# Earlier modulations, and side work begun by a credit of VectorE time, in a two-block transformer kernel

## The reference

```
mod = silu(c) @ w_ada + b_ada                    # 2048 x 12288: sh1, sc1, gt1, sh2, sc2, gt2
h = rmsnorm(x) * (1 + sc1) + sh1
qa, ka, va, qb, kb, vb, q_idx, k_idx, w_idx, ga, gb = split(h @ w_in)
ya = causal attention A (8 heads) @ w_moba_out
yb = attention B (8 heads), keys chosen by an index (top 64 a query) @ w_dsa_out
y = (sigmoid(ga) * ya + sigmoid(gb) * yb) @ w_o
x = x + gt1 * rmsnorm(y);  h = rmsnorm(x) * (1 + sc2) + sh2
x = x + gt2 * rmsnorm(relu(h @ w_ff1)^2 @ w_ff2)
# the second block has two other attentions and a second feed-forward, and no modulation
```

## Time and profile before

| | |
|---|---|
| timed runs | 2645.92, 2650.81, 2651.06 us, median 2650.81 |
| profiled execution | 2645.48 us, span 2643.7 us, mean granted clock 0.99 |
| PE busy | 2572.5 us (97%) |
| DVE busy | 1712.8 us (65%) |
| ACT busy | 1212.1 us (46%) |
| chain that ended last | PE 85%, DVE 10%, ACT 3% |
| HBM read | 563.02 MB, 214 GB/s over the span |

### The profile page before, as it was taken

The page is one execution under the profiler, slowest core; times in us unless marked ns, Lnnn a source line. Parts: engine busy times, 40 slices in busy tenths (PEclk is TensorE's granted clock), DMA queues, the critical chain, the costliest instruction groups (busy, mean ns, idle before and its releaser), DMA issues.

```text
span 2643.7 us, 30528 instructions
## 1 busy us (share of the span) xinstructions
PE 2572.5 (97%) x12368; PEld 2124.6 (80%) x12368; DVE 1712.8 (65%) x2256; ACT 1212.1 (46%) x1766; POOL 5.9 (0%) x15
## 2 busy tenths in 40 slices
PE   6999998999998999999999989999999999999998
PEld 4887786887886888888888878878778888888887
DVE  5897878878885866556556554546655465564555
ACT  3534444534346434434444455445554344443443
POOL 0000000000000000000000000000000000000000
PEclk8999999999999999999999999999999999999999
DMA  8994345788885775555555535534445555555553
GB/s 332 381 348 167 128 150 213 268 339 325 337 328 191 265 292 207 193 189 188 195 188 180 210 131 188 193 129 144 175 151 197 180 188 197 185 191 194 187 193 143
DMA packets 80443, 567.10 MB, mean 215 GB/s; under 512 B 8976, under 2 KB 9104, under 8 KB 15664
## 3 DMA queue, kind: packets, MB, share of 16 engines
q1 hardware_dynamic: 79200, 558.09, 57.8%
q0 software_dynamic: 1104, 7.07, 0.7%
HBM read 563.02 MB, written 2.10 MB: 214 GB/s over the span
## 4 chain that ended last, share of the span: by engine, by line
PE 85%; DVE 10%; ACT 3%; issue 1%; DMA 1%; DVEq 0%; SPq 0%; ACTq 0%
PE ps L884 19%; PE ps L881 19%; PE ps L882 18%; PE ps L925 15%; PE ps L927 8%; DVE wl L1545 4%; DVE ACC L1566 2%; DMA raw<-stream_in 1%; ACT wh L1192 1%; PE ps L941 1%; PE ps L1134 1%; DVE TMP L1671 1%; ACT M L1323 1%; DVE M L1675 1%; PE ps L1110 1%
## 5 line engine op out<-in xcount | busy, mean ns | idle before, releaser
L1545 DVE TENSOR_TENSOR wl<-raw,wh 128x1024 fp32r<-128x1024 f32 x851 | 1003.6, 1220 | 573.3 <-ACT wh L1192 572.8
L1192 ACT ACTIVATE wh<-raw 128x1024 fp32r<-128x1024 f32 x851 | 852.5, 1049 | 726.7 <-PE ps L884 555.1
L925 PE MATMUL ps<-HT,wh 128*128 128x512 f32 x1792 | 634.3, 399 | 0.0
L881 PE MATMUL ps<-wh,U 128*128 128x512 f32 x1376 | 538.1, 391 | 0.0
L884 PE MATMUL ps<-wl,U 128*128 128x512 f32 x1376 | 536.3, 390 | 1.4 <-DVE wl L1545 1.4
L882 PE MATMUL ps<-wh,U 128*128 128x512 f32 x1376 | 535.5, 389 | 0.0
L927 PE MATMUL ps<-HT,wl 128*128 128x256 f32 x1792 | 503.4, 281 | 0.5 <-DVE wl L1545 0.5
L881 PE MATMUL ps<-wh,HT 128*128 128x512 f32 x1120 | 451.0, 403 | 18.7 <-ACT wh L1192 10.2
L884 PE MATMUL ps<-wl,HT 128*128 128x512 f32 x1120 | 445.9, 398 | 12.3 <-DVE wl L1545 12.0
L882 PE MATMUL ps<-wh,HT 128*128 128x512 f32 x1120 | 441.9, 395 | 0.0
L925 PEld LDWEIGHTS ps<-HT,wh 128*128 128x128 f32 x1792 | 336.6, 188 | 83.0 <-DVE M L1912 0.2
(11 more groups left out here) (234 smaller groups left out, 1315.3 us busy)
## 6 DMA issues: line engine op xcount, KB each, us to landing
raw<-stream_in SPq DMA_DIRECT2D x497, 1024.0 KB, 4.8
raw<-stream_in SPq DMA_DIRECT2D x16, 896.0 KB, 7.3
raw<-stream_in SPq DMA_DIRECT2D x17, 640.0 KB, 6.6
raw<-stream_in SPq DMA_DIRECT2D x13, 512.0 KB, 4.7
M<-rows_in POOLq DMA_DIRECT2D x6, 1024.0 KB, 5.9
X<-x_in SPq DMA_DIRECT2D x2, 1024.0 KB, 7.1
y_out<-X SPq DMA_DIRECT2D x4, 512.0 KB, 2.6
CT<-consts_in POOLq DMA_DIRECT2D x1, 376.0 KB, 6.8
```

The lines of the kernel that those rows point to most:

```text
L881: e.matmul(o, ah, H[:, c:c + bw], start=k == k0, stop=False)
L925: e.matmul(o[:, :], H[:, c], a.rearrange("p h n -> p (h n)"), start=k == 0, stop=False)
L1192: e.activation(H, raw[place[n][0]][:, c:c + w], ACT.Copy).then_inc(*hi.tick(p))
L1545: e.tensor_tensor(L, raw[place[n][0]][:, c:c + w], H.bitcast(F32), ALU.subtract).then_inc(*lo.tick(p))
```

## The change

At the start, all four quarters of the second pair's modulation stand ahead of the first chunk's banks on TensorE, and the stream takes the first chunk's load behind two of them; the column sums of that pair come before the last of the four banks. The "a" events take another order of columns and begin in the third phase: eleven there, the other 37 spread over qA to wo0 by a count for each slab. The slabs from qi@2 to wo0 (kiwi apart) write their side steps with `paced()`: a step is written only while a credit is above zero. The credit grows by 1.5 for each piece, shrinks by 2.6 for each modulation load, by a cost for the slab's evacuation and by a cost for each step; at most 4.0 is carried from chunk to chunk. At most two steps are written per chunk. kA's ropes are queued ahead of attention B.

```diff
@@ plan
-    for j in range(2):
-        out += [("p", j, i) for i in range(4)]
-        if j == 0:
-            out.append(chunks.pop(0))
+    out += [("p", 0, i) for i in range(4)] + [("p", 1, 0), ("p", 1, 1), chunks.pop(0), ("p", 1, 2), ("p", 1, 3)]
...
-    mixed(["qi@2", "kiwi", "qB@2", "kB@2", "vB@2", "kA@2", "vA@2"], [], 1)
-    ada = [("a", c, j) for c in (3 * D, 3 * D + 1024, 2 * D, 2 * D + 1024, 4 * D, 4 * D + 1024) for j in range(8)]
-    mixed(["qA", "gb0", "yb0", "gb1", "yb1", "ga0", "ya0", "ga1", "ya1", "wo0", "wo1"], ada, 1, ADA_SKIP, True)
+    chunks = phase(2)
+    chunks.insert(4, ("g", "kiwi", 0))
+    ada = [("a", c, j) for c in (3 * D, 3 * D + 1024, 4 * D, 2 * D, 2 * D + 1024, 4 * D + 1024) for j in range(8)]
+    beside(chunks, ada, (0, 1, 0, 0, 0) + 5 * (1, 1, 0, 0))
+    for name, n in (("qA", 4), ("gb0", 3), ("yb0", 2), ("gb1", 4), ("yb1", 2), ("ga0", 6), ("ya0", 2), ("ga1", 6),
+                    ("ya1", 2), ("wo0", 6), ("wo1", 0)):
+        m = len(slab_chunks(name))
+        beside([("g", name, i) for i in range(m)], ada, [(i + 1) * n // (m - 1) - i * n // (m - 1) if i < m - 1 else 0
+                                                         for i in range(m)])
@@ work_order
+SIDE_COST = {"rope": 2.1, "attention": 0.6, "index": 1.0, "turnx": 0.3, "rot": 1.0, "srow": 2.3}
+EVAC_COST = {"qi": 2.7, "qB": 2.7, "kB": 2.7, "vB": 2.7, "kA": 2.7, "vA": 2.7, "qA": 1.3, "yb": 2.8, "ya": 5.6, "wo": 2.8}
 FIRST_EVAC = {"qA": ("index",), "gb0": ("attention", "B"), "v2": ("attention", "M")}
...
+    def paced():
+
+        while side and side[0][1] == segments(side[0][0]):
+            side.popleft()
+        if side and at["credit"] > 0:
+            at["credit"] -= SIDE_COST.get(side[0][0][0], 0.3)
             steps(1)
...
-            hooks = {(0, nb - 1): lambda: steps(max(1, rate // 2))}
+            hooks = {(0, nb - 1): paced if pace else lambda: steps(max(1, rate // 2))}
...
+            if name.partition("@")[0] in FIRST:
+                for k in pieces[ps[0]]["ks"] + pieces[ps[-1]]["ks"]:
+                    finish("turnx", max(x for x, q in enumerate(X_TILES) if q[0] <= k))
+            for task in NEEDS.get((name, i), ()):
+                finish(*task)
+            if pace:
+                width_us = width / 1024
+                at["credit"] = min(at["credit"], 4.0) + (2.7 - 1.2) * width_us * sum(len(pieces[p]["ks"]) for p in ps)
+                at["credit"] -= 2.6 * (nx - n - many)
+                if i + many == total:
+                    at["credit"] -= EVAC_COST.get(name[:2], 0.0) if name[-2:] != "@0" else 0.0
...
-            if hooks is not tail:
+            if pace:
+                paced()
+            elif hooks is not tail:
                 steps(rate // 2)
...
-    first_mods(0, 0)
-    split(4)
+    first_sums(0, 1, 2, 3)
+    add("rowcopy", 3)
+    colsum(3)
+    first_sums(4)
+    add("xhalves", 0)
+    split(6)
+    first_sums(5, 7, 8)
     for t in range(2):
         for b in range(2):
-            add("bank", "qi@0", parts[4], t, b, True, False)
-    at["done"] = parts[4][-1]
-    first_mods(1, 5)
+            if (t, b) == (1, 1):
+                add("rowcopy", 8)
+                colsum(8)
+            add("bank", "qi@0", parts[6], t, b, True, False)
+    at["done"] = parts[6][-1]
+    add("xhalves", 1)
...
-    run("qi@2")
+    run("qi@2", pace=True)
     later("rope", "qi")
     run("kiwi")
     later("ki")
     later("index")
     for name in FIRST[1:]:
-        run(f"{name}@2", 2)
-    later("rope", "qB")
-    later("rope", "kB")
+        run(f"{name}@2", pace=True)
+    for name in ("qB", "kB", "kA"):
+        later("rope", name)
     later("attention", "B")
-    run("qA", 2)
+    run("qA", pace=True)
     later("rope", "qA")
-    later("rope", "kA")
     later("attention", "A")
     for s in range(2):
-        run(f"gb{s}", 2 - s)
-        run(f"yb{s}")
+        run(f"gb{s}", pace=True)
+        run(f"yb{s}", pace=True)
...
+NEEDS = {("wo0", 4): [("mix", 1)], ("wo0", 7): [("srow", "mix")], ("fd00", 0): [("gm", "f", 0, 0)],
+         ("gd00", 0): [("gm", "g", 0, 0)]}
```

More of the change, by code:

```diff
@@ L27 @@
 RING = 4
-ADA_SKIP = 10
 MAGIC = 12582912.0
@@ L124, in plan @@
     assert not columns
-    mixed(["qi@2", "kiwi", "qB@2", "kB@2", "vB@2", "kA@2", "vA@2"], [], 1)
-    ada = [("a", c, j) for c in (3 * D, 3 * D + 1024, 2 * D, 2 * D + 1024, 4 * D, 4 * D + 1024) for j in range(8)]
-    mixed(["qA", "gb0", "yb0", "gb1", "yb1", "ga0", "ya0", "ga1", "ya1", "wo0", "wo1"], ada, 1, ADA_SKIP, True)
+    chunks = phase(2)
[7 more added lines that the diff above has]
+                                                         for i in range(m)])
+    assert not ada
     mixed([f"f{p}{g}{s}" for g in range(4) for p in "ud" for s in range(2)],
@@ L262, in work_order @@
     side, held, pending, tiles = deque(), deque(), [], deque()
-    at = {"pos": 0, "ring": 0, "done": None}
+    at = {"pos": 0, "ring": 0, "done": None, "credit": 0.0}
     slots = [None] * RING
@@ L283, in finish @@
         while any(t == task for t, _ in side):
+            steps(1)
+    def paced():
[3 more added lines that the diff above has]
+            at["credit"] -= SIDE_COST.get(side[0][0][0], 0.3)
             steps(1)
@@ L338, in evac, with run @@
                 add("product", held.popleft())
-    def run(name, rate=1, head=None, tail=None, room=None, begin=0):
+    def run(name, rate=1, head=None, tail=None, room=None, begin=0, pace=False):
         i, total = begin, len(slab_chunks(name))
@@ L464, in ffn, with first_sums @@
                 later("srow", f)
-    def first_mods(pair, n0):
-        for n in range(n0, n0 + 4):
+    def first_sums(*ns):
+        for n in ns:
             ada(n)
@@ L473, in first_mods @@
                 add("xturn", 1)
-        add("rowcopy", n0 + 3)
-        colsum(n0 + 3)
-        add("xhalves", pair)
-    first_mods(0, 0)
-    split(4)
+    first_sums(0, 1, 2, 3)
[5 more added lines that the diff above has]
+    first_sums(5, 7, 8)
     for t in range(2):
         for b in range(2):
-            add("bank", "qi@0", parts[4], t, b, True, False)
-    at["done"] = parts[4][-1]
-    first_mods(1, 5)
+            if (t, b) == (1, 1):
[4 more added lines that the diff above has]
+    add("xhalves", 1)
     at["pos"] = 9
@@ L499, in work_order @@
     for name in FIRST[1:]:
-        run(f"{name}@2", 2)
-    later("rope", "qB")
-    later("rope", "kB")
+        run(f"{name}@2", pace=True)
+    for name in ("qB", "kB", "kA"):
+        later("rope", name)
     later("attention", "B")
-    run("qA", 2)
+    run("qA", pace=True)
     later("rope", "qA")
-    later("rope", "kA")
     later("attention", "A")
     for s in range(2):
-        run(f"gb{s}", 2 - s)
-        run(f"yb{s}")
+        run(f"gb{s}", pace=True)
+        run(f"yb{s}", pace=True)
     finish("attention", "A")
     add("row", "mix", 0)
-    run("ga0")
-    run("ya0")
+    run("ga0", pace=True)
+    run("ya0", pace=True)
     later("mix", 0)
-    run("ga1")
+    run("ga1", pace=True)
     finish("mix", 0)
-    run("ya1")
+    run("ya1", pace=True)
     add("row", "mix", 1)
@@ L521, in work_order @@
     later("srow", "mix")
-    run("wo0")
+    run("wo0", pace=True)
     run("wo1", tail=tail_hooks(0), room=[("U", 0, 0), ("U", 0, 1)])
```

## The result

The changed kernel takes 2668.16 us (median of four runs, 2667.35 to 2672.14) against 2650.01 (2645.92 to 2651.06): a ratio of 1.008 with a 95% interval of [1.0068, 1.0092], so 0.8% slower. The profiled execution took 2667.35 us, its span 2665.3 against 2643.7, so 21.6 us have to be found. The page's part 1 answers to the earlier trace rows: every engine does as much as before, and TensorE is 1.5 us busier.

What follows compares the result with a forecast made beforehand. TensorE, busy 97% of the span, was taken as the bound, so only its waits and slow clock could change. Terms -3 - 10 + 1 + 5 + 29 - 1 = +21 us gave 2668 us, range 2653 to 2690.

Steps and rivals of the forecast that it cites:

- A: Start: second pair's row products ahead of the banks, next low half at 48.9 not 51.31; -3 us (-5.2 to +1).
- B: 412 to 456 us: ropes and modulations no longer share chunks, waits and slow clock go; -10 us (-11.1 to -7).
- C: Third-phase projections, 204 to 343 us: eleven modulations come in, index steps move later; +1 us (-2.8 to +6).
- D: Beside qA: index steps, splits and modulations give VectorE 56 us against TensorE's 43 and some 5; +5 us (+2 to +8).
- E: gb0's last chunk: attention B forced behind five ropes, 3.5 us per head in a chain; +29 us (24.6 to 36).
- F: 560 to 800 us: at most six modulations in eight chunks, none in the last slab; -1 us (-2 to 0).
- the second: Rival at forced attention B: heads overlap at 1.99 us each, no change overall, 2650 us; chance 0.10.
- The third: Rival: leftover credit finishes ropes and attention B by gb0's last chunk, no forced finish, faster, 2640 us; chance 0.08.
- The fourth: Rival: third phase and qA turn VectorE-bound over 180 us, 30 us lost, about 2693 us in all; chance 0.05.

Runs made afterwards that it cites:

- e1: Kernel before with only the new start (second pair's row products and column sums ahead of the first chunk's last bank): 2643.26 us, ratio 0.9979 to before.
- e7: Kernel before with the new start and the 48 modulation loads spread, none beside qA and gb0's ropes: 2638.01 us, ratio 0.9960 to before.
- e5: Kernel before with the new start, five modulation loads moved beside kA and vA, the others from gb0's seventh chunk on: 2643.08 us, ratio 0.9984 to before.
- e3: Changed kernel with its start and moved loads, but side steps by the old rates and order, no credit: 2652.19 us, ratio 1.0014 to before.
- e6: Kernel before with the new start, attention B held back until gb0's evacuation forces it, no ropes ahead: 2655.54 us, ratio 1.0029 to before.
- e2: Changed kernel with the modulation loads where the kernel before has them, from gb0's third chunk on: 2643.97 us, ratio 0.9984 to before.
- e8: Changed kernel with index and attention steps costing no credit and kA's ropes behind attention B: 2656.13 us, ratio 1.0028 to before.
- e4: Changed kernel with kA's four ropes queued behind attention B: 2661.75 us, ratio 1.0046 to before.

## Why the prediction was right, and where only its sum was

The forecast was 2668 and slower, and the cause is the one that it named: attention B is forced in one piece at the end of gb0. The terms of its sum were off, and in part against each other.

**A, start: forecast -3, measured -6.2.** The first bank starts at 35.01, forecast 34.9. The start of the changed kernel on TensorE (start, us, engine, line; count; idle before and releaser):

```profile
35.01 0.50 PE L915 MATMUL ps<-wh,HT 128*128 128x512 f32 x1
...
39.87 0.61 PE L990 MATMUL ps<-ONES,ACC 128*128 128x1 f32 x4
...
43.08 0.50 PE L915 MATMUL ps<-wh,HT 128*128 128x512 f32 x1 [1.11 <-DVE HT L1665]
...
45.13 0.50 PE L918 MATMUL ps<-wl,HT 128*128 128x512 f32 x1 [1.32 <-DVE wl L1579]
```

From there the forecast was wrong by a miscount: a bank of this chunk is 6 matmuls, so the three banks have 18 and not 36. They end at 39.3, not 43.1; the next low half comes at 45.13, forecast 48.9. The fourth bank no longer covers the chain to the operand halves, and TensorE waits 1.1 and 1.3 us. But the slow slices of 0.73 and 0.71 are 1.00 and 1.00, with one of 0.83 between. The second chunk starts 6.2 us earlier, 1.0 beyond my best case; the other columns of the table, which have the same start, say 5.2 to 6.0 there.

**B, ropes with modulations: forecast -10, measured about -10.** Of the 11.1 us the 7.7 of waiting went wholly, and the clock from 400 to 438 is 0.98, which leaves 0.8. The step was right, but part of what it won only moved: the four ropes of kA left gb0's chunks and stand at the head of E.

**C, third phase: forecast +1, measured about +7.** TensorE is busy 5.0 us less than in the earlier trace rows, and 0.83 in the slice at its end costs 1.7. I priced VectorE's sum over slabs and found room on the whole; it has that room, busy 110.61 of 139 us. But the four waits for evacuations (L1912) are all at the first bank of a slab, and there order decides. VectorE and TensorE at the start of qA:

```profile
334.51 1.85 DVE L1816 SCALAR_TENSOR_TENSOR RT<-ACC,WI,RT 128x128 f32<-128x128 f32 x4 [2.13 <-ACT ACC L1407]
336.28 2.35 DVE L1579 TENSOR_TENSOR wl<-raw,wh 128x1024 fp32r<-128x1024 f32 x2
338.55 2.48 DVE L1912 TENSOR_TENSOR M<-ps,M 128x512 f32<-128x512 f32 x4
...
339.29 0.50 PE L915 MATMUL ps<-wh,HT 128*128 128x512 f32 x1 [2.20 <-DVE M L1912]
```

The loads lie behind a slab's first two chunks, and its last chunk is charged for the evacuation, so the credit lets most index steps of the third phase gather in the third chunk. VectorE stands 2.13 us until ScalarE has such a step's values, and the next chunk's split and the evacuation stand behind it. So it is with the two longest of the four waits, 2.2 us each. Before the third, of 1.65, ScalarE's high half stands 5.2 us behind an index step's copy that waits for TensorE; before the fourth, of 1.05, VectorE has two ropes. Together C lies beyond my bound of +6. Waits of this kind add to 1.8 us in e1, 2.1 in e7, 4.2 in e5 and 5.1 in e3. The longest of them has top-k steps of the index directly ahead on VectorE in e1, e3 and e7, and a modulation in e5.

**D, index beside qA: forecast +5, measured about +8.** 5.7 us idle where there were 0.6, and a clock of 0.95 (0.05 x 55 = 2.8 us). The largest wait is seen on VectorE at the end of qA, where three index steps that were forced and a rope stand ahead of the evacuation that TensorE waits 3.7 us for:

```profile
388.51 0.29 DVE L1824 MAX8 TP<-RT 128x8 f32<-128x128 f32 x1
...
393.18 0.75 DVE L1705 TENSOR_TENSOR TMP<-M,CT 128x256 f32<-128x256 f32 x2
...
395.30 0.68 DVE L1914 COPY M<-ps 128x512 f32<-128x512 f32 x1
```

**E, forced attention B: forecast +29, measured +24.3.** From the last chunk's start (438.00) to yb0 (483.58) it is 45.6 us; less 5.4 for the chunk and 15.9 for eight heads, 24.3 are lost, just under the low end of 24.6. TensorE's gap was forecast 40.5 at the full clock and is 40.0. VectorE and TensorE in that stretch:

```profile
440.94 0.76 DVE L1705 TENSOR_TENSOR TMP<-M,CT 128x256 f32<-128x256 f32 x2
...
449.81 0.28 DVE L1861 CUSTOM_DVE_ANT_0 ACC<-ps,DB 128x128 f32<-128x128 f32 x1
...
454.29 0.29 DVE L1861 CUSTOM_DVE_ANT_0 ACC<-ps,DB 128x128 f32<-128x128 f32 x1 [2.38 <-PE ps L1168]
...
457.80 0.29 DVE L1861 CUSTOM_DVE_ANT_0 ACC<-ps,DB 128x128 f32<-128x128 f32 x1 [0.65 <-PE ps L1168]
...
461.31 0.29 DVE L1861 CUSTOM_DVE_ANT_0 ACC<-ps,DB 128x128 f32<-128x128 f32 x1 [0.98 <-PE ps L1168]
```

Four ropes were forced where I counted five, and scores are first read 11.8 us after the chunk's start, forecast 13.7. From the second link on each takes 3.51 us, forecast 3.5. Two parts of the term were mis-sized. One rope less is 1.9 us. The clock is 3.4: I went four tenths of the way from the full clock to 1.2 GHz throughout, 4.4 us, and only the first link was slow (4.48 us, 0.97 over). Nor did a slow spell of 3.4 us follow, which the upper end has; where one stands alone in a slice, 0.83 from 40 to 50 us, it costs 1.7. The chain by itself has the same price here and in e6. The ropes hold up the first probabilities by 8.0 us (13.96 after the chunk's start, 5.95 in e6); without that and the slow link E is 15.3, and e6 without its two slow spells is 15.1.

By the Trainium skill (TensorE: Matmul & The Clock Gate, section What's actually happening) the throttled state is the default and activity lifts it. That such a burst stays throttled to its end was my reading of it, and the trace doesn't bear that reading out: 0.80 and 0.69 from 440 to 460, then 1.00 with TensorE busy 6.85 and 6.21 of 10 us.

**yb0 and gb1, not forecast: about +2.3.** Attention A begins later and falls into yb0, gb1 and their loads; from 484 to 571 TensorE is busy 84.67 of 87 us, where before it waited for nothing from 464 to 545.

**F: forecast -1, measured -3.1** from ga0 to the end. (At yb1 the start reads 1.7 us later than at ga0, since a column sum that stood behind yb1's first chunk now stands ahead of it.) The table says what it goes with: from ga0 to the end e3, which has the change's loads without its credit, wins 5.9 us; e1, which has neither, loses 0.1, and e2, which has the credit without the loads, loses 2.2. Only a small part is seen in waits for low halves from 560 to 800 us, 1.4 us where there were 2.0.

Read by waits and clock, the terms up to ga0 add to -6.2 - 10.3 + 6.7 + 7.9 + 24.3 + 2.3 = +24.7, which is what the chunk starts say at ga0; with F it is +21.6. Forecast was +21: C and D came out 8.6 higher, yb0 and gb1 2.3, A, B and F 5.6 lower, E 4.7 lower. So that the total came so near is luck: the errors cancel.

Of the rivals, the second (the heads overlap) fell with links of 3.51 us against 1.99. The third was right that without the forced finish the loss is smaller, but its 2640 was wrong: e8, in which nothing is forced, takes 2656. The fourth, a loss to VectorE before gb0, is real at half its price: C and D measure 15 us of its 30. That is what the forecast lacked: C, D and E are not three prices but one shortage, which moves between them.

Left open: by which waits the loads win F, and whether e7 would gain more with other places for its loads behind yb0, so that wo0's column sum falls a chunk later, as in e1. None were tried.

## What to carry to other kernels

Work that is put off by a credit needs its deadline in the count: sum the second engine's time up to the point where something must be finished, and what doesn't fit there comes due in one piece. An attention head here passes from TensorE to VectorE, ScalarE, VectorE and back; such a chain took 3.5 us a head alone, where TensorE spends 2.0 a head between projections, so price the forced form, not the work. A load that brings VectorE work should not fall into chunks that carry ropes (e7). Nor should a side step that waits for another engine stand ahead of an evacuation; this is read from the trace, and no run changes it alone.

## What the runs showed of the hardware that was not expected

The granted clock came back during an intermittent burst. TensorE in the changed kernel's burst, in order of time:

```profile
451.96 0.47 PE L1153 MATMUL ps<-CT,ACC 128*128 128x128 f32 x1 [9.89 <-DVE ACC L1867]
...
456.45 0.33 PE L1153 MATMUL ps<-CT,ACC 128*128 128x128 f32 x1 [0.17 <-DVE ACC L1867]
...
459.96 0.33 PE L1153 MATMUL ps<-CT,ACC 128*128 128x128 f32 x1 [1.21 <-DVE ACC L1867]
```

Behind the standstill of 9.9 us the transposes take 0.47 us, from 456.45 on 0.33, and the granted clock is then 1.00 for twenty microseconds although TensorE waits 1.2 us in nearly every link. In e4, where no wait of the burst is over 1.9 us, all three slices from 440 to 470 show 1.00. But the slice behind e4's burst, in which TensorE is back at the banks, does not:

```profile
470.00:480.00 10.00, 9.89 (x38) 8.14 (x39) 7.82 (x14) 4.56 (x7) 0.54 (x1) 0.83 0.07 21
```

And e6's burst, with waits of the same size, has one slice of 0.83 at its head and one behind it, while behind the changed kernel's the slices from 480 to 500 are at 1.00. So three bursts of this form ran mostly at the full clock, and these traces don't say what decides where a slow spell falls.
